# Two-step recurrence in the first block, with four gate products inside the attention before it

## The reference

```
h = rms_norm(x)*(1+sc)+sh
u, q, k, v, g_s, g_a = split(h @ w_in)        # 512, 3 x 512, 2 x 1024 columns
lam_bar = exp(lam*dt); b_bar = (lam_bar-1)/lam * b
states[s] = lam_bar*states[s-1] + b_bar @ u[s]       # complex, 32 groups of 64 states, 16 channels
y = gelu(real(c @ states) + d*u);  y = y*sigmoid(y @ w_glu)
ya = softmax(q k^T / 8, causal) v                    # 8 heads of 64
merged = sigmoid(g_s)*(y @ w_ssm) + sigmoid(g_a)*(ya @ w_attn)
x = x + gt*rms_norm(merged @ w_out)
```

## Time and profile before

| | |
|---|---|
| median of 3 runs | 2496.75 us (2494.17 to 2502.11) |
| profiled execution | 2497.32 us, span 2495.4 us |
| busy share of the span | PE 83%, DVE 28%, ACT 17%, POOL 4% |
| mean granted clock of TensorE | 0.921 |
| part that the change touches | about 0 to 330 us of the span |

### The profile page before, as it was taken

One profiled execution on the slowest core, in us unless ns is written; L12 is line 12 of the kernel. 1 busy time (PEld: TensorE's weight loads), 2 busy tenths in 40 slices (PEclk: granted clock), 3 DMA queues, 4 the chain that ended last, 5 costly groups with the idle time before them and its releaser, 6 DMA issues.

```text
span 2495.4 us, 24674 instructions
## 1 busy us (share of the span) xinstructions
PE 2082.7 (83%) x9827; PEld 1179.8 (47%) x9828; DVE 707.3 (28%) x1203; ACT 413.0 (17%) x598; POOL 105.1 (4%) x118
## 2 busy tenths in 40 slices
PE   6988689788999788889796697799989686869998
PEld 2644246223333222223232284488558475838873
DVE  2747714211112211112111225100026465431001
ACT  1211011211121221112221211100012221211000
POOL 2000001000000000000000100200000030200000
PEclk9898789999999999999998898999999887989999
DMA  9571254899699999998999951244343200013420
GB/s 347 198 255 54 67 178 148 351 428 426 239 403 428 427 428 427 428 411 338 428 428 428 408 215 67 77 136 168 123 154 116 95 1 1 1 61 118 150 103 18
DMA packets 106378, 578.68 MB, mean 232 GB/s; under 512 B 7055, under 2 KB 8179, under 8 KB 81552
## 3 DMA queue, kind: packets, MB, share of 16 engines
q1 hardware_dynamic: 101008, 562.41, 56.6%
q0 software_dynamic: 5280, 15.10, 2.0%
HBM read 576.41 MB, written 1.07 MB: 231 GB/s over the span
## 4 chain that ended last, share of the span: by engine, by line
PE 69%; DMA 15%; DVE 11%; ACT 4%; issue 2%; DVEq 0%; SPq 0%; ACTq 0%
DMA ring<-in_w_up 13%; PE ps L1729 12%; PE ps L1228 10%; PE ps L1740 6%; PE ps L616 6%; PE ps L624 5%; PE ps L1269 4%; PE ps L1242 3%; PE ps L1290 2%; PE ps L1252 2%; PE ps L527 2%; PE ps L2067 2%; PE ps L2073 1%; DMA ring<-in_ada_w 1%; PE ps L837 1%
## 5 line engine op out<-in xcount | busy, mean ns | idle before, releaser
L1729 PE MATMUL ps<-arena,ring 128*128 128x256 f32 x1408 | 304.4, 379 | 2.0 <-issue 2.0
L1729 PEld LDWEIGHTS ps<-arena,ring 128*128 128x128 f32 x1408 | 267.4, 190 | 38.6 <-issue 2.3
L1228 PE MATMUL ps<-ring,arena 128*64 128x512 f32 x1088 | 241.1, 596 | 0.0
L1269 PE MATMUL ps<-ring,arena 128*32 128x512 f32 x1088 | 151.0, 705 | 66.6 <-DMA ring<-in_w_up 66.4
L1740 PE MATMUL ps<-ring,arena 128*128 128x512 f32 x352 | 151.4, 592 | 0.0
L616 PE MATMUL ps<-arena,ring 128*128 128x256 f32 x672 | 149.0, 384 | 0.7 <-ACT arena L593 0.7
L1228 PEld LDWEIGHTS ps<-ring,arena 128*64 128x64 f32 x1088 | 75.5, 137 | 153.5 <-issue 153.0
L616 PEld LDWEIGHTS ps<-arena,ring 128*128 128x128 f32 x672 | 129.0, 193 | 20.4 <-issue 1.5
L624 PE MATMUL ps<-ring,arena 128*128 128x512 f32 x288 | 130.7, 615 | 3.3 <-ACT arena L2166 2.0
L1242 PE MATMUL ps<-ring,arena 128*64 128x512 f32 x544 | 120.5, 594 | 12.5 <-ACT arena L1191 12.5
L1269 PEld LDWEIGHTS ps<-ring,arena 128*32 128x32 f32 x1088 | 36.1, 127 | 167.7 <-issue 91.4
(11 more groups left out here) (501 smaller groups left out, 2345.9 us busy)
## 6 DMA issues: line engine op xcount, KB each, us to landing
ring<-in_w_gate SPq DMA_DIRECT2D x64, 2048.0 KB, 18.6
ring<-in_w_up SPq DMA_DIRECT2D x64, 2048.0 KB, 22.1
ring<-in_w_down SPq DMA_DIRECT2D x64, 2048.0 KB, 20.0
ring<-in_ffn_w_gate_up SPq DMA_DIRECT2D x22, 2048.0 KB, 7.9
ring<-in_ada_w SPq DMA_DIRECT2D x12, 2048.0 KB, 16.0
ring<-in_ffn_w_down SPq DMA_DIRECT2D x10, 2048.0 KB, 7.9
ring<-in_w_in SPq DMA_DIRECT2D x8, 2048.0 KB, 17.5
ring<-in_dn_w_in SPq DMA_DIRECT2D x6, 2048.0 KB, 7.7
```

Source lines behind the costliest of these rows:

```text
L1228: m = pe.matmul(bank(b)[c * CAP:(c + 1) * CAP, :], xT[:, j * P + h * CAP:j * P + (h + 1) * CAP], w[h][:, j, c * 512:(c + 1) * 512], start= ...
L1269: m = pe.matmul(bank(0)[(2 * i + c) * FEW:(2 * i + c + 1) * FEW, :], XT[:, j * P + h * CAP:j * P + h * CAP + FEW], w[h][:, j, c * 512:(c + ...
L1729: m = pe.matmul(bank(b0 + g)[:, c * SEQ:(c + 1) * SEQ], w[:, k, (2 * g + c) * P:(2 * g + c + 1) * P], hT2[:, k, :], start=(k == 0), stop=( ...
```

## The change

The recurrence advances two times per step. With `mag` squared and the drive of an even time taken as B u[s] + (lam_bar B) u[s-1] (new tiles BL), the scan runs over 128 even times. The outputs of even times come from C and the state; those of odd times from C lam_bar (new tiles CL) and the same state plus a direct term K u of the odd time, where KT is the product of B and C per group, made by 32 small matmul calls ahead of the projections. The tables hold 128 times instead of 256. The forward turn is no longer summed on VectorE: four partial products (`parts`, two sets) go to TensorE, which sums them in PSUM, so an output quarter is 36 calls of 128 columns instead of 8 of 256, and a drive 16 calls of 128 columns instead of 8 of 256. VectorE has ten element-wise operations of 512 columns a quarter instead of twelve of 1024.

Of the eight gate products the four of g_a come first and are computed in the attention: TensorE computes gate u between the scores of u+1 and the transposition of u, in bank 7; ScalarE copies it out before its Exp of unit u, and takes their Sigmoid in place at the start of s3. Both halves of bank 6 take the results of the value product. In s3 four gate products remain, and the branch product of the attention is put ahead of the last output product.

The core of the diff; the angle tables' halving, buffer places of minor weight and unchanged lines are left out:

```diff
@@ -226,7 +226,7 @@
-        pc_gate = [piece(by_k(w_in, (4 + n) * 512, (5 + n) * 512), gate_ps, TT * (n + 1)) for n in range(4)]
+        pc_gate = [piece(by_k(w_in, (4 + m) * 512, (5 + m) * 512), gate_ps, TT * (n + 1)) for n, m in enumerate((2, 3, 0, 1))]
...
-        cosS, sinS = ar3(10240, 4096, SJ), ar3(14336, 4096, SJ)
+        HALF = SEQ // 2
+        cosS, sinS = ar3(14336, 2048, SJ), ar3(16384, 2048, SJ)
         BTr, BTi, CTr, CTi = (ar3(18432 + 512 * n, 512, SQ) for n in range(4))
+        BLr, BLi = (ar3(10752 + 512 * n, 512, SQ) for n in range(2))
+        CLr, CLi = (ar3(13312 + 512 * n, 512, SQ) for n in range(2))
+        KT = ar3(10240, P, SQ)
...
-        BC = [BTr, BTi, CTr, CTi]
+        blam = [ar3(8704 + 256 * n, 256, SJ) for n in range(2)]
+        Bl = [ar(10240, 512), ar(11776, 512)]
+        BC = [BTr, BTi, CTr, CTi, BLr, BLi]
...
-        sA, sB, sT, sU = ar3(0, 1024, 4), ar3(1024, 1024, 4), ar3(4096, 1024, 4), ar3(5120, 1024, 4)
+        sA, sB, sT = (ar3(512 * n, 512, 4) for n in range(3))
+        parts = [[ar3(a, 512, 4) for a in of] for of in ((4096, 4608, 5120, 5632), (1536, 11776, 12288, 12800))]
...
-            for n in range(4):
+            for n in range(6):
                 act.wait_ge(bc_ps, n + 3)
                 o(act.copy(BC[n], bank(6 + n % 2).rearrange("p (q m) -> p q m", q=SQ)), bc_ev)
...
+            o(dve.tensor_tensor(mag, mag, mag, ALU.mult))
+            o(dve.tensor_copy(lr, lbr))
-            o(dve.tensor_tensor(bbar[1], bbar[1], btmp, ALU.add))
+            o(dve.scalar_tensor_tensor(bbar[1], bbar[1], -1.0, btmp, ALU.mult, ALU.subtract))
+            lrb, lib = cols_bc(lr, SSM_C), cols_bc(lbi, SSM_C)
+            o(dve.tensor_tensor(blam[0], bbar[0], lrb, ALU.mult))
+            o(dve.tensor_tensor(btmp, bbar[1], lib, ALU.mult))
+            o(dve.tensor_tensor(blam[0], blam[0], btmp, ALU.add))
+            o(dve.tensor_tensor(blam[1], bbar[1], lrb, ALU.mult))
+            o(dve.tensor_tensor(btmp, bbar[0], lib, ALU.mult))
+            o(dve.tensor_tensor(blam[1], blam[1], btmp, ALU.subtract))
...
+            for n in range(2):
+                o(dve.tensor_tensor(Bl[n].rearrange("p (j g c) -> p j g c", g=2, c=SSM_C),
+                                    spread(blam[n], [SSM_C, SJ], [0, 2], [1, SSM_C]), mb, ALU.mult), bc_ready)
...
-            dve.wait_ge(bc_ps, 6)
-            steps = spread(con("steps"), [0, 4], [1, SEQ])
-            for h in range(4):
-                f3, t3 = sinS[:, 4 * h:4 * h + 4, :], cosS[:, 4 * h:4 * h + 4, :]
+            steps = spread(con("steps"), [0, 8], [2, HALF])
+            for h in range(2):
+                f3, t3 = sinS[:, 8 * h:8 * h + 8, :], cosS[:, 8 * h:8 * h + 8, :]
...
+            dve.wait_ge(bc_ev, 6)
+            ctr, cti, clr, cli, tmp = (x.rearrange("p q (j c) -> p (q j) c", j=4) for x in (CTr, CTi, CLr, CLi, ar3(3072, 512, SQ)))
+            lrb, lib = cols_bc(lr, 2 * SSM_C), cols_bc(lbi, 2 * SSM_C)
+            o(dve.tensor_tensor(clr, ctr, lrb, ALU.mult))
+            o(dve.tensor_tensor(tmp, cti, lib, ALU.mult))
+            o(dve.tensor_tensor(clr, clr, tmp, ALU.subtract))
+            o(dve.tensor_tensor(cli, ctr, lib, ALU.mult))
+            o(dve.tensor_tensor(tmp, cti, lrb, ALU.mult))
+            o(dve.tensor_tensor(cli, cli, tmp, ALU.add))
...
-            for n in range(4):
+            for n in range(6):
                 pe.wait_ge(bc_ready, n + 3)
                 if n >= 2:
                     pe.wait_ge(bc_ev, n - 1)
-                src = (Bd + Cd)[n]
+                src = (Bd + Cd + Bl)[n]
...
-            pe.wait_ge(bc_ev, 4)
+            pe.wait_ge(bc_ev, 6)
+            for q in range(SQ):
+                for n in range(2):
+                    for j in range(4):
+                        m = pe.matmul(bank(6)[32 * j:32 * j + 32, 32 * q:32 * q + 32], Bd[n][:, 128 * q + 32 * j:128 * q + 32 * j + 32],
+                                      (CTr, CTi)[n][:, q, 32 * j:32 * j + 32], start=(n == 0), stop=(n == 1),
+                                      tile_position=(0, 32 * j), skip_group_check=True)
+            m.then_inc(bc_ps, 1)
             pe_cols(pe, arrived(pe, pc_in[0]), 4, hT, KD, proj_ps)
+            pe.wait_ge(bc_ev, 7)
             pe_cols(pe, arrived(pe, pc_in[1]), 6, hT, KD, proj_ps)
...
+            act.wait_ge(bc_ps, 9)
+            o(act.copy(KT, bank(6)[:, 0:P].rearrange("p (q m) -> p q m", q=SQ)), bc_ev)
             act_tables(act, o, 0)
             act.wait_ge(proj_ps, 1)
             o(act.copy(uT.rearrange("p c s -> p (c s)"), bank(4, 2)), proj_ev)
             for n, raw in enumerate((qraw, kraw)):
-                act_tables(act, o, 1 + n)
+                if n == 0:
+                    act_tables(act, o, 1)
                 act.wait_ge(proj_ps, 2 + n)
                 o(act.copy(raw, bank(6 if n == 0 else 0, 2)), proj_ev)
-            act_tables(act, o, 3)
             act.wait_ge(proj_ps, 4)
             o(act.copy(vN.rearrange("p t n -> p (t n)"), bank(2, 2)), proj_ev)
...
+        def pv_bank(n):
+            return bank(6)[:, SEQ * (n % 2):SEQ * (n % 2 + 1)] if n < len(U1) else bank(6 + n % 2)[:, 0:SEQ]
+
...
-            if n >= 2:
-                pe.wait_ge(pv_ev, n - 1)
+            if n >= 2 or n == 1:
+                pe.wait_ge(pv_ev, n if n < len(U1) else n - 1)
             for i in range(HPG):
                 for kb in range(2):
                     r = HD * (i % 2)
-                    m = pe.matmul(bank(6 + n % 2)[r:r + HD, (i // 2) * P:(i // 2 + 1) * P], v_of(kb, i),
+                    m = pe.matmul(pv_bank(n)[r:r + HD, (i // 2) * P:(i // 2 + 1) * P], v_of(kb, i),
...
+        def pe_gate(pe, i, b):
+
+            n, t = i // TT, i % TT
+            w = arrived(pe, pc_gate[n])
+            for k in range(KD):
+                m = pe.matmul(bank(b), hT[:, k, t * P:(t + 1) * P], w[:, k, :], start=(k == 0), stop=(k == KD - 1))
+            m.then_inc(gate_ps, 1)
+
+        def gate_at(i):
+            n, t = i // TT, i % TT
+            return (sga if n < 2 else sgs)[:, t, (n % 2) * 512:(n % 2 + 1) * 512]
...
             for u, (g, t) in enumerate(U1):
                 if u + 1 < len(U1):
                     scores(u + 1)
+                if u:
+                    pe.wait_ge(gate_ready, u)
+                pe_gate(pe, u, 7)
                 pe_probs(pe, u, u, lambda kb, i: vN[:, kb, (HPG * g + i) * HD:(HPG * g + i + 1) * HD])
 
         def act_s4(act, o):
             for u in range(len(U1)):
+                act.wait_ge(gate_ps, u + 1)
+                o(act.copy(gate_at(u), bank(7)), gate_ready)
                 act_probs(act, o, u, u)
...
-                for n, m_ in enumerate((BTr, BTi)):
+                for n, (now, last) in enumerate(((BTr, BLr), (BTi, BLi))):
+                    at_ = n * HALF
                     for j in range(4):
-                        m = pe.matmul(bank(j)[:, n * SEQ:(n + 1) * SEQ], m_[32 * j:32 * j + 32, q, :],
-                                      uT[32 * j:32 * j + 32, q, :], start=True, stop=True, tile_position=(32 * j, 0))
+                        pe.matmul(bank(j)[:, at_:at_ + HALF], now[32 * j:32 * j + 32, q, :],
+                                  uT[32 * j:32 * j + 32, q, :].rearrange("p (s r) -> p r s", r=2)[:, 0, :],
+                                  start=True, stop=False, tile_position=(32 * j, 0), skip_group_check=True)
+                    for j in range(4):
+                        m = pe.matmul(bank(j)[:, at_ + 1:at_ + HALF], last[32 * j:32 * j + 32, q, :],
+                                      uT[32 * j:32 * j + 32, q, :].rearrange("p (s r) -> p r s", r=2)[:, 1, 0:HALF - 1],
+                                      start=False, stop=True, tile_position=(32 * j, 0), skip_group_check=True)
                 m.then_inc(bu_ps, 1)
...
             def gate(i):
-
-                n, t = i // TT, i % TT
-                if i >= 2:
+                if i >= 6:
                     pe.wait_ge(gate_ready, i - 1)
-                w = arrived(pe, pc_gate[n])
-                for k in range(KD):
-                    m = pe.matmul(bank(4 + t), hT[:, k, t * P:(t + 1) * P], w[:, k, :], start=(k == 0), stop=(k == KD - 1))
-                m.then_inc(gate_ps, 1)
+                pe_gate(pe, i, 4 + i % TT)
 
             def y_of(q):
                 pe.wait_ge(st_ready, q + 1)
                 if q >= 2:
                     pe.wait_ge(y_ready, q - 1)
                 for j in range(4):
-                    for n, (c_, x_) in enumerate(((CTr, sT), (CTi, sU))):
-                        m = pe.matmul(bank(6 + q % 2)[32 * j:32 * j + 32, 0:SEQ], c_[:, q, 32 * j:32 * j + 32], x_[:, j, :],
-                                      start=(n == 0), stop=(n == 1), tile_position=(0, 32 * j))
+                    y2 = bank(6 + q % 2)[32 * j:32 * j + 32, 0:SEQ].rearrange("p (s r) -> p r s", r=2)
+                    for r, (cr_, ci_) in enumerate(((CTr, CTi), (CLr, CLi))):
+                        for n, x_ in enumerate(parts[q % 2]):
```

(64 more changed lines are left out.)

11 lines of the change are left out of this document (6 added, 5 removed).

## The result

Six executions of each kernel: before 2498.19 us (2494.17 to 2502.11), after 2506.26 us (2501.77 to 2509.06). The ratio is 1.0033, 95% interval 1.0020 to 1.0046, so the change makes the kernel slower by about 8 us. That lies inside the range of 2484 to 2512 us, but the forecast was "no change", 2496 us.

A forecast was written before the change was run, and what follows sets the result against it. VectorE bounded the recurrence; after the change TensorE would. With the attention's +37.2 us included, the glu product came 3.5 us earlier; with +2.5 for KT and projections, -1.0 on 2497.3 gave 2496 us, range 2484 to 2512.

The forecast's parts named there:

- KT: Small products on TensorE after the turn, before the projections: 3.8 us for 64 records, bounds 2.2 and 7.4 us.
- the output product: Recurrence, TensorE: 72 records with partial overlap between column strips, 4.1 us each, four times; bounds 2.5 and 7.9 us.
- the clock behind the Gelu: Glu product, starting after an idle stretch on TensorE: a loss of 1.0 us, as the branch product had.
- The ring: Attention, each later unit's loop through TensorE, ScalarE and VectorE, gate included: 19.5 us; 16.1 at full clock, 20.1 at half.
- the Gelu is bare: End of the recurrence: the branch product no longer covers the Gelu, so 3.1 us lie open before the glu product.
- rival B: Recurrence: a strip's output products run one after another, 7.9 us instead of 4.1, +15.2 us, 2511 us; chance 0.25.
- KT and projections: TensorE before the attention: small products cost 3.8 us, projections may regain part at better clock; net +2.5, from +1 to +7.4.
- Nothing differs after it: All stages after the glu product: unchanged apart from shifting with it, 0 us.
- A: The forecast itself: 43 us saved in the recurrence and 37 us spent in the attention cancel, 2490 to 2503; 0.55 with E.
- C: Attention: TensorE keeps full clock, -9, 2487 us; with output products at their lower bound 2481 us; chance 0.17.
- D: Attention: gates fill idle TensorE time, only the first delays the Exp, +5 there, 2464 us; chance 0.03.
- E: Recurrence, VectorE: scans keep their time despite half the columns, 2496 to 2499 us; chance counted with A, 0.55.

The follow-up runs named there:

- the run of ScalarE's order: Changed kernel, but in the attention ScalarE does Exp and the copy of the transposed probabilities before copying the gate out of PSUM; 2473.5 us, ratio 0.9902.
- The halved branch: Changed kernel with the attention's branch product cut in two halves of 7 us and the last output product between them; 2500.2 us, ratio 1.0004.

## Why the prediction was wrong, point by point

The step that failed is one term of TensorE's sum in the recurrence, the output product: put at 4.1 us, it took 6.3, four times on the engine that bounds the stage. The three runs with other orders of its calls show that the long runs on one column strip make the difference. Two smaller terms push the same way, the clock behind the Gelu and a stretch of block two that was put at nothing; the projections push against.

**Attention, right.** Forecast 77.3 us (+37.2), measured 77.5 (+37.4). The ring was put at 19.5 and measured 19.3 and 19.9; the small products at half clock, the gates between 7.62 and 8.19.

**Recurrence, bound right, one term wrong.** TensorE is the bound and VectorE has room, as said; the Gelu is bare by 3.2 us, forecast 3.1. The term that failed is the output product: 4.1 us, measured 6.3, four times, +8.6 us. Its bounds, 2.5 and 7.9, held, and rival B named the mechanism and the point from which it decides, 6.2 us; the measured value lies just past that point, and so does the result past 0.3%. I weighted it by L814's runs of four, which say nothing of runs of sixteen, although I had seen that difference in the diff. The drives came out shorter (2.0 and 1.1 us against 2.5 and 1.5), the first gate 7.9 for 8.4 (the row that the forecast names, 257.27, has 8.24). Sum forecast 70.6 with the Gelu, measured 76.5. VectorE came out as forecast: its last product ends at 297.7 us, ten before TensorE asks for it. The fixed part of its products is 0.20 us by the forecast's own figures, not 0.16, which would change nothing.

The rule of the Trainium skill ("TensorE: Matmul & The Clock Gate", Part 3, What overlaps and what doesn't), that matmuls keep program order at start and end, would let a run of r records on a strip hold the next strip back by r-1 of them. With the 0.11 us a record of the forecast that gives, as an estimate, 3.5, 5.3, 6.2 and 6.6 us for runs of two, four, eight and sixteen (not rival B's 7.9, as the prediction had it). Measured are 1.96, 2.02, 4.33 and 5.95: all shorter, and no other price a record would fit all four, so the trace does not agree with strict order, least of all for short runs. But for the run of sixteen it came near, and I gave it too little weight.

**KT, mis-sized.** Forecast 3.8 us for 64 records, measured 0.76 (88.58), and 1.08 in five of eleven executions. Even my lower bound of 2.2 was too high: it halved L814's price though the data were an eighth as many columns.

**Projections, sign wrong.** I had +2.5 us net for KT and projections, it is -2.5 in both executions of the changed kernel. The two extra turns of B-tiles (L580) lie directly ahead of the turn of h; L614 then ran at full clock (1.13 and 1.09 us against 1.97 each in the kernel before), and the granted clock of the projections was 1.00 where the earlier trace rows show 0.94 (windows of the changed kernel, columns as in the earlier trace rows):

```profile
89.28:130.82 41.54, 41.54 (x199) 36.58 (x193) 23.17 (x25) 7.80 (x8) 0.00 (x0) 1.00 0.29 102
```

But the same turns of B-tiles did not bring this every time. In five of the eleven executions the second half of the turn and the KT products ran at half clock and the stage took 81.9 us, here in the run of ScalarE's order (TensorE's timeline):

```profile
86.14 1.97 PE L614 MATMUL ps<-constants,arena 128*128 128x128 f32 x8 [1.49 <-DVE arena L634]
88.83 1.08 PE L661 MATMUL ps<-arena 128*32 128x32 f32 x64 [0.73 <-ACT arena L621]
89.84 43.14 PE L644 MATMUL ps<-arena,ring 128*128 128x256 f32 x192
```

What decides between the two was not found.

**Behind the glu product, clock underrated.** I allowed 1.0 us for its start at falling clock; the product took 9.90 us instead of 7.07, and the w_ssm product after it 16.74 us, 1.0 more than before: +4.3 us from glu to the router, forecast +1.0 with the glu product's loss. The halved branch gives 7.07 back. The same gap went with 7.14, 8.83 and 9.90 us in different kernels, so it has no single price, and this one is not explained by the gap alone.

**"Nothing differs after it", not quite.** Block two, whose code is unaltered, takes 1066.6 to 1067.3 us in all eleven profiled executions of kernels with the two-step recurrence and 1064.7 and 1064.8 in the two with the old one. Most of the difference sits in one place, three products that ran at full clock in the two and at half in the eleven, in TensorE's timeline of the changed kernel:

```profile
2184.32 2.93 PE L2161 MATMUL ps<-arena 128*128 128x128 f32 x12 [2.41 <-ACT arena L2252]
2188.19 2.93 PE L2165 MATMUL ps<-arena 128*128 128x128 f32 x12 [0.94 <-ACT arena L2254]
2190.91 2.77 PE L2167 MATMUL ps<-arena 128*128 128x128 f32 x12
```

Their counterparts in the kernel before took 1.60, 1.60 and 1.50 us: 3.9 us in sum, of which the rest of block two gives 1.5 back. Why the clock falls there in these kernels was not found; two executions with the old recurrence are also few.

**Sum.** Forecast and measured, stage by stage: preparation and projections +2.5 against -2.5, attention +37.2 against +37.4, recurrence -41.7 against -35.8, behind glu +1.0 against +4.3, block two 0 against +2.4. That is -1.0 against +5.8. The terms that came out dearer sum to 11.8 us; that the total is off by 6.8 only is luck, the 5.0 us of KT and projections, of which half is missing in five of eleven executions. The 2 us left to the medians' 8.1 stay open; the stretches that differ between executions of one kernel, the projections among them, are where they could lie.

**The rivals.** A's balance of 43 us saved and 37 us spent did not hold: 36 and 37. B happened in part, and with the small terms it decided. C's condition, full clock in the attention, did not occur in the changed kernel but did as soon as the wait was gone. The prediction's argument against C misread a row: in the kernel before a transposition stood at full clock after 2.17 us of idle time too, not only after the shortest (TensorE's timeline):

```profile
193.43 1.09 PE L700 MATMUL ps<-constants,arena 128*128 128x128 f32 x8 [2.17 <-DVE arena L736]
```

D was refused for the right reason, ScalarE's order. E is refuted, a scan run of eight takes 3.63 us where eight of the earlier trace rows took 5.5.

## What to carry to other kernels

When work is moved onto an idle engine, follow its result too: here the copy of four gate products out of PSUM stood ahead of a link of the critical chain on ScalarE's queue, and the attention grew by 37.4 us for 28.5 us of work; with the copy behind that link it grew by 8.6 us, and the move was worth 19 us. Before pricing a product in column strips by an existing row, compare the number of records that follow one another on one strip. And a gap on TensorE can cost twice, the gap itself and the half clock of what follows it; the second part varied here between nothing and 2.8 us for one and the same gap.

## What was unexpected of the hardware

- Records of different 32-column strips overlap almost fully in runs of two and four on a strip (1.96 and 2.02 us for 64 records of 128 columns) and only in part in runs of eight and sixteen (4.33 and 5.95 us).
- 64 records (32 calls) of 32 columns of weights and 32 of data take 0.76 to 1.08 us, 0.012 to 0.017 us a record.
- The same code ahead of the projections, TensorE's stage of turn, KT and projections, took 79.4 us in six executions and 81.9 in five, with its first products at full or at half clock.
- The same gap of 3.16 us before the same product went with 7.14, 8.83 and 9.90 us for it.
- In the attention an idle stretch of 4.6 us a ring, beside one of 1.16, went with half clock for three products in every ring; a ring with the one of 1.15 us alone kept full clock throughout.
